# The heads of C in every second unit, and two keys on a partition in the values of B

## The chip, the cores and the metric

The kernel is one program on one NeuronCore of a Trainium2 chip. Five engines run their own instruction streams and wait for each other through semaphores: TensorE (PE, the matrix engine), VectorE (DVE), ScalarE (ACT), GpSimd (POOL) and SyncE (SP), which here only issues DMAs. TensorE reads SBUF and writes PSUM, eight banks of 512 f32 columns on 128 partitions. The metric is the device time of one execution in microseconds; lower is better. The profile is of one execution of its own.

## The reference, cut to what matters

Two layers of a decoder run over 256 prompt tokens and over 8 sequences of 8 new tokens, each with 1024 past positions. Token mixing has three head groups, A (6 heads, dilated window), B (6 heads, keys chosen by an indexer) and C (4 heads, two softmax maps each). The new tokens attend over caches; those of B and C lie in pages of 128 positions:

```python
def paged_rows(pool):
    rows = pool[l, page_table]
    return rows.reshape((nb, past) + rows.shape[3:])
...
kc_all = jnp.concatenate([paged_rows(cache_c_k), kc], axis=1)
vc_all = jnp.concatenate([paged_rows(cache_c_v), vc], axis=1)
oc = diff_attend(qc, kc_all, vc_all, q_pos, lam_l, lam_init, subln_g_l, rel_bias)
...
s = jnp.einsum('bthmd,bshmd->bhmts', q.astype(jnp.float32) * D_C ** -0.5, k_all.astype(jnp.float32))
s = jnp.where(dist >= 0, s + bias[None, :, None], -jnp.inf)
p = jax.nn.softmax(s, axis=-1)
...
a = p[:, :, 0] - lam_full * p[:, :, 1]
o = jnp.einsum('bhts,bshd->bthd', a, v_all.astype(jnp.float32))
```

A and B are of the same shape, with one map: softmax of q times the keys plus a bias, times the values. The order of the positions within a softmax and its sum of values doesn't matter, as long as both use the same. All is f32.

## The kernel before, in words

A layer runs in this order: projections (`PROJ`), with tiles of the adaLN matmuls between them; the units, which are the subject here; the output projection (`mix_out`, L1386) and norm; the MLP (L1085, L1524). All tiles of weights come through a ring of four slots on SP's queue.

**Units.** The 16 units of a layer (`UNITS`) do the new tokens' attention over the caches. Units 0 to 7 take the six heads of A for sequence n, units 8 to 15 (`second`) the six of B for sequence n - 8. A chunk is 128 features, that is two heads; a unit has three chunks of A or B and, as the fourth, one of the two chunks of C: heads 0 and 1 beside A, 2 and 3 beside B. A chunk's queries are 32 columns (`G`) of `qs`, gathered by GpSimd and zero where a head's features aren't, so that one matmul does both heads.

- `turn(u)` (L1297, L1298, L1306): TensorE transposes the exponentiated logits `S`, eight pages of 128 keys and the new keys, into PSUM; ScalarE (first pass) or VectorE (second) copies them to `ptbuf` (`turned_unit`).
- `logits(u+1)` (L1277): for each half of the keys (`q` 0 and 1) four matmuls of 512 columns, one for each chunk, into partitions 32c to 32c + 31 (`psf[G * c:G * c + G]`); then, as `q` 2, four of 8 columns for the new keys, after a wait for `u_nset`. For B the selection is added by L1284, one matmul for each chunk and q.
- one item of the prompt's attention (L1366, L1351, L1376), of which `SLOTS` says which unit takes which.
- `values(u)` (L1321): for each page and the new keys (`vs`) four matmuls of 128 columns into partitions 32c to 32c + 31 of bank 3.
- in the first seven units half of a late projection tile (L1397), `turn_out` (L1328), the other half. Before each waits `i_logit`, the item's maxima from VectorE.
- `turn_out(u)` waits for `u_oset`, which VectorE's `read_outputs` gives (L1830, L1832, L1834: the sum's reciprocal, and the output scaled by it), and turns the outputs back; VectorE's `place_outputs` copies them to `oT` and frees the bank for the next turn.

SP issues the loads of a unit's keys when the logits of unit n - 2 are through, and of its values when the values of n - 2 are; there are two buffers for everything, `s` = n mod 2. C's pages are read in rows of 512 bytes, half of the 1024 bytes that a position has, since a unit takes one chunk of two; ScalarE issues some of these loads in the second pass.

`LATE` has eight projection tiles; tile 0 is done ahead of unit 0, tile n + 1 in unit n. At the program's start three matmuls at L1149 make the bias table: the first two write partitions 0 to 15 of bank 0 and of bank 1, with 512 columns each, the third partitions 32 to 47 with 135 columns (`dist_ps_at`).

```python
def dist_ps_at(c):

    p0, (u0, u1) = 32 * (c // 2), DIST[c]
    return bank[c % 2][p0:p0 + H, 0:u1 - u0]
```

## Time and profile before

| | |
|---|---|
| median of 3 runs | 1382.98 us (1381.21 to 1383.24) |
| profiled execution | 1387.83 us |
| its span in the profile | 1386.0 us, 23151 instructions |
| TensorE busy | 1300.4 us, 94% |
| VectorE, ScalarE, GpSimd busy | 496.0, 258.4, 59.6 us |
| read from and written to HBM | 354.20 MB, 58.40 MB |

A row of a view gives the line, the engine, the operation, out<-in by names, stationary rows*columns, moving rows x columns, the type and the number of records. A matmul of f32 leaves two MATMUL records, a transpose one. Records of one line that follow each other are merged in a timeline; its second number is the stretch from the first's start to the last's end, so the distance between two rows' starts says best how long a group took. In a record's duration is also the time through the array, so concurrent and pipelined records overlap. `PEclk` is the granted clock as a share of 2.4 GHz.

### The profile page before, as it was taken

Reading aid. Unit: us, or ns where it says so; the run is one execution under the profiler, and the core shown is the slowest. Engines: PE = TensorE matmul, PEld = TensorE weight load, DVE = VectorE, ACT = ScalarE, POOL = GpSimd, SP = SyncE. Lnnn points to the kernel's source line nnn. Section 1 sums busy time; section 2 is a strip of 40 time slices with the busy share of each in tenths; the row PEclk is TensorE's granted clock in tenths of the full one; section 3 lists DMA queues with packets and bytes.
Section 4 is the critical chain, followed back from the end, with each engine's and each line's share of the span. In section 5 each row is a group of like instructions: output and inputs, shape, how many; then the busy total and the mean of one; then the engine's idle time right before and its main releaser. Section 6 shows DMA issues by size and latency. Waiting matters only on the chain.

```text
span 1386.0 us, 23151 instructions
## 1 busy us (share of the span) xinstructions
PE 1300.4 (94%) x8038; PEld 809.5 (58%) x8038; DVE 496.0 (36%) x1444; ACT 258.4 (19%) x647; POOL 59.6 (4%) x265
## 2 busy tenths in 40 slices
PE   5988899988999999999999999999899999999998
PEld 2544356644566666666666444665456667767775
DVE  1102458876664111011112056777756411101113
ACT  0111124422213110000003212443220311100001
POOL 1000000000001000000001000000000100000000
PEclk9999899998999999999999999999899999999999
DMA  9989989999943768877863687999994366676663
GB/s 350 226 277 260 274 292 370 329 333 347 300 167 111 277 232 299 314 272 262 331 222 138 205 292 276 332 331 349 349 349 173 129 244 212 221 284 212 212 212 137
DMA packets 189646, 363.83 MB, mean 262 GB/s; under 512 B 22928, under 2 KB 140440, under 8 KB 187866
## 3 DMA queue, kind: packets, MB, share of 16 engines
q1 hardware_dynamic: 155040, 345.62, 72.4%
q10 hardware_dynamic: 34490, 16.74, 5.0%
q8 instruction: 64, 1.05, 0.3%
q14 instruction: 52, 0.43, 0.1%
HBM read 354.20 MB, written 58.40 MB: 298 GB/s over the span
## 4 chain that ended last, share of the span: by engine, by line
PE 76%; DVE 9%; DMA 6%; DVEq 3%; issue 2%; ACT 2%; SPq 2%; ACTq 0%
PE psf L1085 22%; PE psf L1524 19%; DMA ring<-in_tiles 5%; PE psf L1386 4%; PE psf L1436 4%; PE psf L1321 3%; PE psf L1277 3%; PE psf L1507 3%; PE psf L1102 2%; PE psf L1397 2%; PE psf L1132 1%; PE psf L1351 1%; PE psf L1164 1%; DVE ranks L1708 1%; DVEq L1711 1%
## 5 line engine op out<-in xcount | busy, mean ns | idle before, releaser
L1085 PE MATMUL psf<-hT,ring 128*128 128x320 f32 x1184 | 328.8, 437 | 3.5 <-DMA ring<-in_tiles 3.2
L1085 PEld LDWEIGHTS psf<-hT,ring 128*128 128x128 f32 x1184 | 224.0, 191 | 111.2 <-issue 15.9
L1524 PE MATMUL psf<-big,ring 128*128 128x320 f32 x1024 | 278.9, 433 | 4.1 <-DVE big L1981 2.1
L1524 PEld LDWEIGHTS psf<-big,ring 128*128 128x128 f32 x1024 | 193.5, 190 | 90.4 <-issue 5.5
L1981 DVE TENSOR_TENSOR big<-sq 128x320 f32<-128x320 f32 x64 | 31.5, 492 | 248.8 <-ACT sq L1054 248.5
L1622 DVE TENSOR_SCALAR rstd<-psf,adaT 128x256 f32<-128x256 f32 x32 | 15.4, 482 | 250.1 <-PE psf L1524 234.9
L1012 ACT ACTIVATE sq<-xT 128x320 f32<-128x320 f32 x32 | 15.0, 470 | 321.5 <-DVE xT L1626 321.5
L1386 PE MATMUL psf<-oT,ring 128*128 128x320 f32 x256 | 71.6, 435 | 2.2 <-DVE oT L1844 1.0
L1054 ACT ACTIVATE sq<-psf 128x320 f32<-128x320 f32 x64 | 28.0, 437 | 238.9 <-PE psf L1085 224.6
L1277 PE MATMUL psf<-big,qs 128*32 128x512 f32 x512 | 66.7, 616 | 3.7 <-ACT zT L858 2.2
L1321 PE MATMUL psf<-big,ptbuf 128*32 128x128 f32 x2048 | 65.9, 283 | 0.1
L1436 PE MATMUL psf<-ring,hT 128*128 128x512 f32 x128 | 62.2, 631 | 0.0
L1102 PE MATMUL psf<-ring,cz 128*32 128x512 f32 x336 | 49.5, 626 | 12.9 <-DVE cz L1558 8.7
L1386 PEld LDWEIGHTS psf<-oT,ring 128*128 128x128 f32 x256 | 47.8, 190 | 23.5 <-DVE xT L1626 1.8
L1321 PEld LDWEIGHTS psf<-big,ptbuf 128*32 128x32 f32 x2048 | 56.4, 114 | 7.1 <-issue 4.4
L1569 DVE TENSOR_REDUCE adaT<-psf 128x36 f32<-128x144 f32 x24 | 7.3, 304 | 140.6 <-PE psf L1112 140.1
L1792 DVE CUSTOM_DVE_ANT_0 S<-psf,sbias 128x1032 f32<-128x1032 f32 x32 | 39.3, 1229 | 38.2 <-PE psf L1277 18.6
L858 ACT ACTIVATE zT<-psf,zscale 128x320 f32<-128x320 f32 x40 | 20.7, 528 | 162.1 <-PE psf L1085 70.3
L1708 DVE MAX8 ranks<-workbuf 128x8 f32<-128x520 f32 x64 | 44.9, 702 | 3.8
L1710 DVE MATCH_REPLACE8 workbuf<-ranks,workbuf 128x520 f32<-128x520 f32 x64 | 43.8, 684 | 0.3 <-issue 0.3
L1436 PEld LDWEIGHTS psf<-ring,hT 128*128 128x128 f32 x128 | 24.2, 200 | 31.6 <-issue 31.6
L1507 PE MATMUL psf<-hT,big 128*128 128x320 f32 x128 | 38.2, 463 | 2.9 <-ACT hT L1029 2.9
(212 smaller groups left out, 1303.3 us busy)
## 6 DMA issues: line engine op xcount, KB each, us to landing
ring<-in_tiles SPq DMA_DIRECT2D x266, 512.0 KB, 4.7
big<-in_cache_a SPq DMA_DIRECT2D x64, 768.0 KB, 7.2
out_cache_a<-in_cache_a SPq DMA_DIRECT2D x64, 768.0 KB, 6.2
big<-in_pool_bk SPq DMA_DIRECT2D x128, 192.0 KB, 5.3
big<-in_pool_bv SPq DMA_DIRECT2D x128, 192.0 KB, 6.9
big<-in_pool_cv SPq DMA_DIRECT2D x192, 64.0 KB, 5.4
big<-in_pool_ck SPq DMA_DIRECT2D x128, 64.0 KB, 4.5
big<-in_pool_ck ACTq DMA_DIRECT2D x128, 64.0 KB, 5.3
```

Source lines behind the costliest of these rows:

```text
L1085: ins = pe.matmul(ps[:, 0:T], ring[:, s, k, :], rhs[:, k, :], start=k == 0, stop=k == KD - 1)
L1102: ins = pe.matmul(bank[3][G * g:G * g + G, :], cz[:, c, :], wide(tile, kk), start=c < 4, stop=c >= 4)
L1277: ins = pe.matmul(psf[G * c:G * c + G, 512 * q:512 * q + w], qs[:, u.s, G * c:G * c + G], rhs, start=True, stop=not masked)
L1321: ins = pe.matmul(bank[3][G * c:G * c + G, 0:P], lhs, rhs, start=j == 0, stop=j == NPG)
L1386: ins = pe.matmul(wo_bank(m)[:, 0:T], ring[:, s, k, :], oT[:, AT_O[k], :], start=k == 0, stop=k == KD - 1)
L1436: ins = pe.matmul(bank[v_bank(g, tt)], hT[:, 2 * s + kk, P * tt:P * tt + P], wide(ring[:, slot], kk), start=first, stop=last)
L1507: ins = pe.matmul(up_bank(m)[:, 0:T], spare[m][:, k, :], hT[:, k, :], start=k == 0, stop=k == KD - 1)
L1524: ins = pe.matmul(bank[6 + m % 2][:, 0:T], ring[:, s, k, :], uT[:, KD * q + k, :], start=q + k == 0, stop=q == 3 and k == KD - 1)
L1708: dve.max(eight, work)
L1710: dve.match_replace(work, eight, work, TAKEN)
L1792: dve.tensor_tensor_reduce(out=S[:, 0, :], in0=psf[:, 0:L], in1=sbias[u.second][:], scale=1.0, scalar=-3e38, op0=ALU.add, op1=ALU.max, acc ...
L1981: dve.tensor_tensor(uT[:, i, :], sq[:, i % 2, :], sq[:, i % 2, :], ALU.mult).then_inc(up_set.sem, 1)
```

## The change

A unit is now light (n even) or heavy (n odd). A light unit has the three chunks of A or B alone, on 64 rows of queries; a heavy one these and both chunks of C, for its own sequence, on 128 rows. In the second pass the sequences are swapped in pairs (`n % NB ^ 1`), so that each sequence is heavy once. The table `QUAD` gives the 32 partitions of a chunk's result: chunks 0 and 2 share partitions 0 to 31, chunk 1 has 32 to 63, and C's two chunks 64 to 95 and 96 to 127. In the logits chunk 2 accumulates on chunk 0's result, its queries lying in other rows; in the values it gets a bank of its own, bank 4, same partitions.

C has one buffer for keys and one for values, loaded for heavy units only, in whole rows of 1024 bytes; GpSimd gathers C's queries for these alone. In the second pass the page of values, of B and of C, is read as 64 partitions with two neighbouring positions each (`load_rows`: 3072 and, for C, 2048 bytes in one piece); two pages fill 128 partitions, and the turn takes the odd and even columns of `S` apart (`page`). The first pass reads the values of A and C, and both passes all keys, in the plain order.

Further edits: tile 1 of `LATE` is done ahead of unit 0 too, so unit n takes tile n + 2; the first unit with two items is 10 and not 11; the C heads' norm (`gn`) is split in prompt and new tokens and not by chunk; the bias rows of C are loaded with one DMA for two maps; and the wait for the free output bank stands ahead of the lower half's turn only in heavy units, in light ones ahead of the values. The diff's core (`...` where lines are left out):

```diff
+C_W = NPG * 2 * P
+QUAD = [0, 1, 0, 2, 3]
+Q_STEP, Q_ROWS = 40, [0, G, 2 * NT]
...
-        self.n, self.b, self.s, self.second = n, n % NB, n % 2, n >= NB
-        self.q, self.k, self.qc, self.kc = (QB, KB, QC + 1, KC + 1) if self.second else (QA, KA, QC, KC)
-        self.v, self.vc = (VB, VC + P) if self.second else (VA, VC)
+        self.n, self.s, self.second, self.heavy = n, n % 2, n >= NB, n % 2 == 1
+        self.b = n % NB ^ 1 if self.second else n
+        self.q, self.k = (QB, KB) if self.second else (QA, KA)
+        self.v = VB if self.second else VA
...
-SLOTS = [*([n] for n in range(11)), [11, 12], [13], [14], [15], [ITEMS]]
+        self.chunks = [0, 1, 3, 4, 2] if self.heavy else [0, 1, 2]
+        self.rows = P if self.heavy else 2 * G
+        self.q_at = 3 * G if self.heavy else 0
+        self.at = 2 * A_W if self.heavy else 0
+    def q_of(self, c):
+        at = self.q_at + ((0, Q_STEP, 2 * G)[c] if c < 3 else G * c)
+        return slice(at, at + G)
...
+SLOTS = [*([n] for n in range(10)), [10, 11], [12], [13], [14], [15], [ITEMS]]
...
+            def load_rows(l, at, pool, dst, signal):
+                for j in range(NPG):
+                    sp.dma_start(dst[64 * (j % 2):64 * (j % 2) + 64, j - j % 2:j - j % 2 + 2, :]
+                                 .rearrange("p e w -> p (e w)"),
+                                 pool[ds(at[j] + l * N_PHYS, 1)].rearrange("o (p e) w -> (o p) (e w)", e=2)
+                                 ).then_inc(signal, 16)
...
             def load_b(l, u, at, half):
-                load_pages(l, at, a["pool_bv" if half else "pool_bk"], 0, (k_in, v_in)[half][u.s], (ld_k, ld_v)[half][u.s])
...
+                if half:
+                    load_rows(l, at, a["pool_bv"], v_in[u.s], ld_v[u.s])
+                else:
+                    load_pages(l, at, a["pool_bk"], k_in[u.s], ld_k[u.s])
...
-                    if d in (6, 7):
-                        at = pages(0, CHECKED) if d == 6 else at
-                        load_c(l, UNIT[0], at, d - 6)
...
-                        load_c(l, UNIT[1], at, d - 13)
+                        load_c(l, at, d - 13)
...
-                        load_c(l, u, at, 0)
...
+                        if u.heavy:
+                            load_c(l, at, 0)
...
-                    load_c(l, then, was, 1, range(NPG // 2 if then.second else NPG))
+                        if then.heavy:
+                            load_c(l, was, 1)
...
-                        for c in range(4):
...
+                        for c in u.chunks:
                             if q < 2:
                                 rhs = (k_in[u.s][:, 4 * q:4 * q + 4, P * c:P * c + P] if c < 3
-                                       else ck_in[u.s][:, 4 * q:4 * q + 4, :])
+                                       else ck_in[:, 4 * q:4 * q + 4, P * (c - 3):P * (c - 3) + P])
...
-                                rhs = zT[:, u.k + c if c < 3 else u.kc, t0:t0 + NT]
-                            masked = u.second and c < 3
-                            ins = pe.matmul(psf[G * c:G * c + G, 512 * q:512 * q + w], qs[:, u.s, G * c:G * c + G], rhs,
-                                            start=True, stop=not masked)
-                            if q == 2 and not masked:
-                                ins.then_inc(u_s.sem, 1)
+                                rhs = zT[:, u.k + c if c < 3 else KC + c - 3, t0:t0 + NT]
+                            masked, g = u.second and c < 3, G * QUAD[c]
+                            ins = pe.matmul(psf[g:g + G, 512 * q:512 * q + w], qs[:, u.q_of(c)], rhs,
+                                            start=c != 2, stop=c != 0 and not masked)
+                            if q == 2 and c and not masked:
...
-                            for c in range(3):
+                            for g in (0, G):
...
-                                ins = pe.matmul(psf[G * c:G * c + G, 512 * q:512 * q + w], selB[half, u.b, :],
+                                ins = pe.matmul(psf[g:g + G, 512 * q:512 * q + w], selB[half, u.b, :],
...
-                    pe.sem_inc(passed, 1)
-                    z0 = TS - NT - NT * u.b
-                    for j in range(NPG // 2, NPG):
-                        pe.transpose(bank[3 + j // 4][:, P * (j % 4):P * (j % 4) + P], S[:, 0, P * j:P * j + P], ident[:])
-                    pe.transpose(bank[2][0:TS, 256:384], znew[:, z0:z0 + TS], ident[:])
-                    if u.n:
-                        pe.wait_ge(u_out.sem, u_out.free(l, u.n))
-                    else:
+                    if u.n == 0:
                         pe.wait_ge(z_set.sem, z_set.done(l, MADE_AT[LATE[0]]))
                     pe.sem_inc(passed, 1)
+                    r, z0 = u.rows, TS - NT - NT * u.b
+                    page = lambda j: (S[0:r, 0, 2 * P * (j // 2) + j % 2:2 * P * (j // 2) + 2 * P:2] if u.second
+                                      else S[0:r, 0, P * j:P * j + P])
+                    for j in range(NPG // 2, NPG):
+                        at = P * j - 512 if u.heavy else r * j
+                        ins = pe.transpose(bank[4][:, at:at + r], page(j), ident[0:r, 0:r])
+                    pe.transpose(bank[2][0:TS, 256:256 + r], znew[0:r, z0:z0 + TS], ident[0:r, 0:r])
+                    if u.heavy:
+                        pe.wait_ge(u_out.sem, u_out.free(l, u.n))
+                        pe.sem_inc(passed, 1)
                     for j in range(NPG // 2):
-                        ins = pe.transpose(bank[3 + j // 4][:, P * (j % 4):P * (j % 4) + P], S[:, 0, P * j:P * j + P], ident[:])
+                        ins = pe.transpose(bank[3 if u.heavy else 4][:, r * j:r * j + r], page(j), ident[0:r, 0:r])
                     ins.then_inc(u_tp.sem, 1)
...
                 def values(u):
...
                     pe.wait_ge(u_tset.sem, u_tset.done(l, u.n))
+                    if u.n == 0:
+                        pe.wait_ge(z_set.sem, z_set.done(l, MADE_AT[LATE[1]]))
+                    elif not u.heavy:
+                        pe.wait_ge(u_out.sem, u_out.free(l, u.n))
...
-                        for c in range(4):
+                        for c in u.chunks:
+                            g = G * QUAD[c]
                             if j < NPG:
-                                lhs = PT[:, j, G * c:G * c + G]
-                                rhs = v_in[u.s][:, j, P * c:P * c + P] if c < 3 else cv_in[u.s][:, j, :]
+                                lhs = ptbuf[:, u.rows * j + g:u.rows * j + g + G]
+                                rhs = v_in[u.s][:, j, P * c:P * c + P] if c < 3 else cv_in[:, j, P * (c - 3):P * (c - 3) + P]
                             else:
-                                v0 = u.v + P * c if c < 3 else u.vc
-                                lhs, rhs = PT[0:TS, j, G * c:G * c + G], vs[0:TS, v0:v0 + P]
-                            ins = pe.matmul(bank[3][G * c:G * c + G, 0:P], lhs, rhs, start=j == 0, stop=j == NPG)
-                            if j == NPG:
-                                ins.then_inc(u_o.sem, 1)
+                                v0 = u.v + P * c if c < 3 else VC + P * (c - 3)
+                                lhs, rhs = PT[0:TS, j, g:g + G], vs[0:TS, v0:v0 + P]
+                            ins = pe.matmul(bank[4 if c == 2 else 3][g:g + G, 0:P], lhs, rhs, start=j == 0, stop=j == NPG)
+                            if j == NPG and c:
+                                ins.then_inc(u_o.sem, 1 if u.heavy else 2)
...
                 def turn_out(u):
                     pe.wait_ge(u_oset.sem, u_oset.done(l, u.n))
-                    pe.matmul(bank[3][:, P:P + 64], osb[:], turnO[:], start=True, stop=True).then_inc(u_ot.sem, 1)
+                    r, w = u.rows, 10 * NT if u.heavy else 4 * NT
+                    pe.matmul(bank[3][:, 256:256 + w], osb[0:r, 0:P], turnO[0:r, 0:w], start=True, stop=True)
+                    pe.matmul(bank[3][:, 256 + 4 * NT:256 + 6 * NT], osb[0:r, P:2 * P], ident[0:r, 2 * NT:G],
+                              start=True, stop=True).then_inc(u_ot.sem, 1)
...
-                chunk(MID[l][0], late_bank(0), hT)
+                pe.wait_ge(ada_set, 1 + max(ada_group(t) for t in PROJ[l] if t[0] in ("mix", "mlp")))
+                for i in range(2):
+                    chunk(MID[l][i], late_bank(i), hT)
...
-                    if u.n + 1 < len(LATE):
+                    if u.n + 2 < len(LATE):
...
-                        i = u.n + 1
+                        i = u.n + 2
...
                 def read_outputs(u):
...
-                    dve.tensor_scalar(osb[:], bank[3][:, 0:P], rs[:, u.s, 0:1], par_all[:, l, P_COEF:P_COEF + 1],
-                                      ALU.mult, ALU.mult).then_inc(u_oset.sem, 1)
+                    dve.tensor_scalar(osb[r, 0:P], bank[3][r, 0:P], rs[r, u.s, 0:1], par_all[r, l, P_COEF:P_COEF + 1],
+                                      ALU.mult, ALU.mult)
+                    dve.tensor_scalar(osb[0:G, P:2 * P], bank[4][0:G, 0:P], rs[0:G, u.s, 0:1], None, ALU.mult
+                                      ).then_inc(u_oset.sem, 1)
...
-                        first = bank[3][q, P + NT * half:P + NT * half + NT]
-                        ins = dve.tensor_copy(oT[q, u.o:u.o + 4, t0:t0 + NT],
-                                              bass.AP(first.tensor, first.offset, [list(first.ap[0]), [2 * NT, 4], [1, NT]]))
+                        turned = bank[3][q, 256:256 + 10 * NT].rearrange("p (c e t) -> p c e t", e=2, t=NT)[:, :, half]
+                        if u.heavy:
+                            dve.tensor_copy(oT[q, 3:8:4, t0:t0 + NT], turned[:, 3:5])
+                        ins = dve.tensor_copy(oT[q, u.o:u.o + 3, t0:t0 + NT], turned[:, 0:3])
```

How the instructions stand. TensorE in the first pass of layer 0, before: the end of unit 1's turn, the logits of unit 2, an item's turn and logits, the values of unit 1.

```order
L1298 MATMUL psf<-ident,znew 64x128
L1306 MATMUL psf<-ident,S 128x128 x4
L1277 MATMUL psf<-big,qs 32x512 x8
L1277 MATMUL psf<-zT,qs 32x8 x4
L1366 MATMUL psf<-ident,S 128x128 x2
L1351 MATMUL psf<-zT 128x256 x4
L1321 MATMUL psf<-big,ptbuf 32x128 x32
L1321 MATMUL psf<-vs,ptbuf 32x128 x4
```

TensorE at the same place in the changed kernel, from the logits of unit 2, a light one; the values are those of unit 1, a heavy one.

```order
L1313 MATMUL psf<-big,qs 32x512 x6
L1313 MATMUL psf<-zT,qs 32x8 x3
L1414 MATMUL psf<-ident,S 128x128 x2
L1399 MATMUL psf<-zT 128x256 x4
L1366 MATMUL psf<-big,ptbuf 32x128 x40
L1366 MATMUL psf<-vs,ptbuf 32x128 x5
```

TensorE one unit on: the turn of light unit 2, the logits of heavy unit 3, an item, and the values of unit 2.

```order
L1338 MATMUL psf<-ident,S 128x64 x4
L1339 MATMUL psf<-ident,znew 64x64
L1345 MATMUL psf<-ident,S 128x64 x4
L1313 MATMUL psf<-big,qs 32x512 x10
L1313 MATMUL psf<-zT,qs 32x8 x5
L1414 MATMUL psf<-ident,S 128x128 x4
L1399 MATMUL psf<-zT 128x128 x2
L1366 MATMUL psf<-big,ptbuf 32x128 x24
L1366 MATMUL psf<-vs,ptbuf 32x128 x3
```

What moved: of eight cache logits in each unit six stand in a light one and ten in a heavy one, of 32 cache values 24 and 40, and a light unit's turn moves 64 columns.

TensorE in the second pass of layer 0, before: the logits of unit 13 with the selection's matmuls (`sel`, `selB`).

```order
L1277 MATMUL psf<-big,qs 32x512 x4
L1284 MATMUL psf<-sel,selB 32x512 x3
L1277 MATMUL psf<-big,qs 32x512 x4
L1284 MATMUL psf<-sel,selB 32x512 x3
L1277 MATMUL psf<-zT,qs 32x8 x4
L1284 MATMUL psf<-sel,selB 32x8 x3
```

The same in the changed kernel, unit 13 being heavy.

```order
L1313 MATMUL psf<-big,qs 32x512 x5
L1320 MATMUL psf<-sel,selB 32x512 x2
L1313 MATMUL psf<-big,qs 32x512 x5
L1320 MATMUL psf<-sel,selB 32x512 x2
L1313 MATMUL psf<-zT,qs 32x8 x5
L1320 MATMUL psf<-sel,selB 32x8 x2
```

What moved: the logits of a half of the keys are five (in a light unit three), and the selection's matmuls two and not three.

VectorE in the second pass of layer 0, before: `read_outputs` and the start of `place_outputs` of unit 10.

```order
L1830 TENSOR_TENSOR rs<-sm 128x1
L1832 RECIPROCAL rs<-rs 128x1
L1834 TENSOR_SCALAR osb<-psf,rs,par_all 128x128
L1844 COPY oT<-psf 64x4x8 x2
```

The same in the changed kernel, unit 10 being light.

```order
L1883 TENSOR_TENSOR rs<-sm 64x1
L1885 RECIPROCAL rs<-rs 64x1
L1887 TENSOR_SCALAR osb<-psf,rs,par_all 64x128
L1889 TENSOR_SCALAR osb<-psf,rs 32x128
L1901 COPY oT<-psf 64x3x8 x2
```

What moved: a second scaled copy, of 32 partitions, stands between the first and the placing.

## Rows read from the trace of the kernel before

**Rows 1.** The page: busy us and share of each engine; the chain's shares.

```profile
PE 1300.4 (94%) x8038; PEld 809.5 (58%) x8038; DVE 496.0 (36%) x1444; ACT 258.4 (19%) x647; POOL 59.6 (4%) x265
...
PE 76%; DVE 9%; DMA 6%; DVEq 3%; issue 2%; ACT 2%; SPq 2%; ACTq 0%
```

**Rows 2.** Timeline of TensorE, a unit of the first pass: start, stretch, group.

```profile
208.75 0.60 PE L1297 MATMUL psf<-ident,S 128*128 128x128 f32 x4
...
209.82 1.92 PE L1277 MATMUL psf<-big,qs 128*32 128x512 f32 x16
211.57 0.22 PE L1277 MATMUL psf<-zT,qs 128*32 128x8 f32 x8
211.72 0.44 PE L1366 MATMUL psf<-ident,S 128*128 128x128 f32 x2
...
213.51 1.95 PE L1321 MATMUL psf<-big,ptbuf 128*32 128x128 f32 x64
215.40 0.42 PE L1321 MATMUL psf<-vs,ptbuf 64*32 64x128 f32 x8
215.75 0.44 PE L1376 MATMUL psf<-adarow,vp 128*64 128x128 f32 x4
```

**Rows 3.** Groups by shape: busy us, mean ns | idle before them, releasers.

```profile
L1277 PE MATMUL psf<-big,qs 128*32 128x512 f32 x512 | 66.7, 616 | 3.7 <-ACT zT L858 2.2 <-DVE sel L1744 1.5
L1321 PE MATMUL psf<-big,ptbuf 128*32 128x128 f32 x2048 | 65.9, 283 | 0.1
...
L1834 DVE TENSOR_SCALAR osb<-psf,rs,par_all 128x128 f32<-128x128 f32 x32 | 13.1, 410 | 2.5
...
L1328 PE MATMUL psf<-turnO,osb 128*128 128x64 f32 x64 | 12.3, 273 | 10.1 <-DVE osb L1834 10.1
...
L1397 PE MATMUL psf<-hT,oT 128*128 128x320 f32 x32 | 9.6, 442 | 1.2 <-DVE nmxi L1862 1.2
L1397 PE MATMUL psf<-hT,wki 128*128 128x320 f32 x32 | 9.6, 442 | 2.1 <-DVE nmxi L1862 2.1
L1397 PE MATMUL psf<-hT,zT 128*128 128x320 f32 x32 | 9.6, 442 | 1.8 <-DVE nmxi L1862 1.8
...
L1277 PE MATMUL psf<-zT,qs 128*32 128x8 f32 x256 | 7.6, 180 | 4.0 <-DVE ptbuf L1908 4.0
```

**Rows 4.** Windows: stretch, length, busy PE PEld DVE ACT POOL, PEclk, DMA share, GB/s.

```profile
38.90:40.80 1.90, 1.90 (x11) 0.37 (x14) 1.18 (x3) 0.00 (x0) 0.00 (x0) 1.00 0.33 93
...
208.70:302.20 93.50, 87.34 (x1084) 56.01 (x1083) 72.86 (x242) 36.35 (x106) 9.03 (x48) 0.98 1.03 344
302.20:373.40 71.20, 63.16 (x803) 35.48 (x803) 47.14 (x166) 18.65 (x59) 4.51 (x24) 0.90 1.09 347
...
320.90:325.20 4.30, 4.30 (x75) 3.11 (x75) 0.90 (x6) 2.01 (x6) 0.00 (x0) 0.50 1.10 350
...
960.00:1045.00 85.00, 75.45 (x952) 43.48 (x946) 58.59 (x205) 21.50 (x69) 5.65 (x30) 0.92 1.07 341
```

**Rows 5.** Line L1149, ns min/median/max and forms; then the group in TensorE's timeline.

```profile
L1149 PE MATMUL psf<-big,relb x6: 275/589/600, 38.9 to 40.2; 34*16 34x512 f32 x4, 34*16 34x135 f32 x2
...
38.92 1.89 PE L1149 MATMUL psf<-big,relb 34*16 34x512 f32 x6
```

**Rows 6.** Timeline of TensorE, the selection's matmuls in a unit of B.

```profile
304.48 0.39 PE L1284 MATMUL psf<-sel,selB 64*32 64x512 bf16 x3
304.80 1.06 PE L1277 MATMUL psf<-big,qs 128*32 128x512 f32 x8
```

**Rows 7.** Timeline of TensorE, the values of two units of B.

```profile
308.92 1.95 PE L1321 MATMUL psf<-big,ptbuf 128*32 128x128 f32 x64
...
321.02 3.64 PE L1321 MATMUL psf<-big,ptbuf 128*32 128x128 f32 x64
```

**Rows 8.** The page, DMA queues (q1 by SP, q10 by ACT): packets, MB, share of 16 engines.

```profile
q1 hardware_dynamic: 155040, 345.62, 72.4%
q10 hardware_dynamic: 34490, 16.74, 5.0%
```

183 lines of the change are left out of this document (98 added, 85 removed).

## The prediction, as it was made

> **What bounds the kernel now.** I read the busy times and the chain of waits first. TensorE is busy 94% of the span and 76% of the chain that ended last is its own; VectorE is busy 36% [rows 1]. So I go to TensorE's timeline in the stretch that the change rewrites, the 16 units of each layer (197 to 386 us and 865 to 1052 us). A unit there is a train of TensorE groups with hardly a gap: turn 1.07 us (208.75 to 209.82), cache logits 1.75, logits of the new keys 0.15, the prompt item, cache values 1.89, new values 0.35 [rows 2]. All groups of the logits waited 3.7 and 4.0 us in the whole kernel, the values 0.1 us, and no DMA is among the releasers [rows 3]. The DMA engines are full there (share 1.03 and 1.09 of their time), but TensorE is busy 87.34 of 93.50 us and 63.16 of 71.20 us [rows 4]. The units run at TensorE's pace, with the transfers just ahead.
>
> **What the matmuls cost there.** Logits and values are matmuls with a stationary operand of 32 columns, so each fills one of four column strips of the array; where its result lies (partitions 0 to 31, 32 to 63, ...) says which. A matmul of f32 leaves two records. Eight cache logits of 512 columns (16 records, two for each strip and half of the keys, four a strip) take 1.75 us by their starts [rows 2]: 0.437 us for each record of a strip, four strips side by side. What happens when two such matmuls want the same strip is shown by the group at L1149: two of its three matmuls write partitions 0 to 15 of two different banks, with 512 columns each, that is four records in one strip, and the group takes 1.89 us at a full clock [rows 4, 5]. Take off the end of the last record, 0.59 us by the group's own records, and three steps of 0.43 us are left. Its third matmul lies in the next strip and adds nothing. So different strips overlap, and the same strip is a queue, whatever the bank.
>
> **The change, part by part.** *Logits.* Before, a unit puts one chunk on each strip. After, a light unit has chunks 0, 1, 2 on strips 0, 1, 0, and a heavy one chunks 0, 1, 3, 4, 2 on strips 0, 1, 2, 3, 0 (the table QUAD). Both have two rounds in strip 0 where there was one. The number of matmuls stays 8 in two units; the rounds double. Four records more in strip 0 at 0.437 us: +1.74 us a unit. The eight-column matmuls of the new keys took 0.15 us; a second round is between 0.05 and 0.15, I take 0.08.
> *Values.* 32 matmuls of 128 columns, 16 records a strip, take 1.89 us, 0.118 a record [rows 2]. Now 32 records stand in strip 0. If the strip sets the pace they take twice 1.89; if issue did, only the streamed columns count, 0.437 times 128/512 = 0.109 a record, 3.49 in all. So +1.60 to +1.89; I take 1.75, between these close ends. The new values took 0.35 us; a second round costs from two records (0.22) to 0.35, I take the lower, since 0.35 holds the change of form too. Together 1.74 + 0.08 + 1.75 + 0.22 = 3.79 us a unit, bounds 3.61 and 4.13, for 32 units: **+121.3 us** (115.5 to 132.2). All of it lies on TensorE, which nothing covers.
> *Masks.* In the units of B the selection's matmuls fill three strips side by side in 0.32 us (304.48 to 304.80) [rows 6]; now two, one round as before: 0.
> *Turns.* The 16 light units transpose 64 rows, not 128. Nine transposes take 1.07 us. At best half goes, 0.53 us; at worst nothing, since the stationary side keeps its 128 columns. I take 0.25: -4.0 us (0 to -8.5). By the Trainium skill (TensorE: Matmul & The Clock Gate, "LDWEIGHTS (loading the stationary operand)") a load's time goes by its columns and not by its rows, so 64 rows would load as slowly as 128. By that alone this term would be nearer 0 and the sum up to 4 us higher; no row here has a transpose of 64 rows.
> *Turning the outputs back.* A second matmul of 16 columns follows the first: at most the 0.15 us of the four eight-column ones, at least two records' 0.04; I take 0.10, +3.2 us. VectorE gets a second scaled copy of the output, 32 x 128, behind one of 410 ns [rows 3]. It raises the signal only after the second. TensorE waits for that signal in 16 units (10.1 us), those with no late projection tile around the turn-back; now there are 18, because one late tile moves ahead of the units. Bounds 0 and 0.41 us each; I take 0.3: +5.4, and 10.1/16 = 0.6 us for each of the two new ones, +1.2. In the other units two half tiles of 2.2 us hide it. Heavy units place two more heads' rows with two more copies; only the next light unit's values wait for that, some 5 us later: 0.
> *Waits that the longer trains swallow.* The second round gives 1.7 us before the eight-column logits wait for the turned new keys: 4.0 us go. It gives 2 us before the late tiles of home wkibuf, zT and oT wait for the item's maxima: 2.1 + 1.8 + 1.2 = 5.1 us go. The wait for the last projected tile, 2.2, and the one for the selection, 1.5, ahead of the first unit of B go too, since that tile comes a unit earlier and VectorE has more time [rows 3]. Together -12.8. What is late next is TensorE itself.
> *Clock.* Of 302 to 373 us the mean granted clock is 0.90, of 960 to 1045 us 0.92; within it stretches at 1.2 GHz, as 320.9 to 325.2, where the values took 3.64 us and not 1.95 [rows 4, 7]. They cost some 0.10 x 71 + 0.08 x 85 = 14 us in all, and the engine had idled ahead of them. With some of the idling gone I take -4 (0 to -14).
> *Transfers.* The bytes are the same; C comes as 1024-byte rows, and B's and C's values as longer runs. Nothing waits for a cache load, and each unit lasts longer: 0. C's buffer is now single, but a load starts when the last heavy unit's logits are through, two units (20 us or more) ahead of use. C for unit 0 is gone and that for unit 1 is double, ahead of the values' projection: -3 to +3, I take 0. POOL gathers less for light units, off the path.
> Sum: 121.3 - 4.0 + 3.2 + 6.6 - 12.8 - 4 = **+110.3 us**. The profiled execution took 1387.83 us, with a span of 1386.0; it becomes 1498. The median of the runs lies 4.85 below it, so the forecast is 1382.98 + 110.3 = **1493 us**. With all ends one way the sum is 115.5 - 8.5 + 1.3 - 12.8 - 14 - 3 = +79, or 1462; the other way, with half of the waits left, 132.2 + 4.8 + 8.6 - 6.4 + 3 = +142, or 1525.
>
> **Rivals.** *The strips are not what counts.* If two matmuls on one strip and different banks overlapped, or strip 0's second round slipped beside the next chunks, the change would keep the saved waits and turns alone: about -12, 1371. The L1149 group speaks against it, and strip 0 alone has twice the records.
> *The transfers set the units' pace (faster).* The queue issued by ScalarE has 34490 packets of 485 bytes on average in 5.0% of 16 engines' span, 32 ns each or 66 ns a kilobyte; the main queue pays 72.4% for 345.62 MB, 46 ns [rows 8]. C's 33.6 MB at the second rate and not the first save 0.66 ms of engine time, 41 us over 16 engines. If the share over 1 were the bound, the kernel would take 1342. It decides only where TensorE would wait for a load, and it waits for none; at +3.8 us a unit it waits still less. Of the 512-byte rows the Trainium skill (DMA: Bandwidth & Descriptors, "Specifications") says that 512 bytes already reach the line rate; by that even these 41 us would not be there, while the two queues' rates differ here by a third.
> *The clock falls in the light units.* In them one or two of four strips work for most of 7.5 us. If the chip then grants 1.2 GHz, as in [rows 7], each light unit loses up to 7.5 us; over half of the 16 it is 60 us, 1553. For it: nothing here shows how the clock takes an array three quarters empty. Against: L1149 ran so at a clock of 1.00, if only for 1.9 us.
> *More is hidden than I count*: other stalls shrink, light trains let items run beside them: 1440 to 1462.
>
> **How the numbers follow.** Forecast (1462 to 1525) 0.77, more hidden 0.06, clock 0.10, strips free 0.04, transfers 0.03. The range of 8 in 10 is 1460 to 1528. A measurement of this kernel can tell about 0.2% from no change. Faster by more: both last cases, 0.07. Within 0.2%: 0.01. Slower: 0.92.
>
> **What would show it.** In the profile after: cache logits of a unit 3.5 us by their starts in light and heavy units alike, values 3.5 to 3.8, the L1149 group unchanged; no wait of the logits for the turned new keys; the wait ahead of the turn-back near 0.9 us; units of 15 to 16 us in the first pass; a DMA share clearly under 1 in the units. Values of 1.9 us, or logits of 1.75, would prove the strips' rule wrong; a mean clock under 0.9 from 200 to 320 us would be the clock's case; a wait for ck, cv, k or v on TensorE would show that I misjudged the single buffer.

## The result, and the profile after

| | before | after |
|---|---|---|
| median, side by side | 1382.10 us (1376.99 to 1383.24, 4 runs) | 1507.51 us (1502.12 to 1510.52, 4 runs) |
| profiled execution, its span | 1387.83, 1386.0 us | 1502.12, 1500.3 us |

The ratio is 1.0911, with a 95% interval of 1.0868 to 1.0954: 125 us slower, against 110 forecast (1493, range 1460 to 1528). The profiled executions are 114.3 us apart, and the sum by steps below is made against these.

The page of after, its lines that answer [rows 1, 8]: busy times, the chain, the two queues.

```profile
PE 1416.1 (94%) x8054; PEld 886.3 (59%) x8054; DVE 499.8 (33%) x1501; ACT 253.9 (17%) x639; POOL 48.8 (3%) x202
...
q1 hardware_dynamic: 119216, 341.68, 67.8%
q10 hardware_dynamic: 21226, 20.93, 6.2%
...
PE 85%; DMA 8%; DVE 3%; issue 2%; ACTq 1%; DVEq 1%; SPq 1%; ACT 1%
```

TensorE has 116 us more of busy time with nearly as many records (8054 and 8038). The timeline of TensorE answers [rows 2]: a light unit's turn, the logits of the heavy unit behind it (20 records), the light unit's values, and later the heavy unit's values.

```profile
203.14 0.46 PE L1338 MATMUL psf<-ident,S 64*128 64x64 f32 x4
...
203.83 3.19 PE L1313 MATMUL psf<-big,qs 128*32 128x512 f32 x19
...
207.49 1.07 PE L1399 MATMUL psf<-zT 32*128 32x128 f32 x8
208.49 3.68 PE L1366 MATMUL psf<-big,ptbuf 128*32 128x128 f32 x48
212.10 0.62 PE L1366 MATMUL psf<-vs,ptbuf 64*32 64x128 f32 x6
...
215.00 0.41 PE L1374 MATMUL psf<-turnO,osb 64*128 64x32 f32 x2
215.25 0.37 PE L1375 MATMUL psf<-ident,osb 64*128 64x16 f32 x2
215.55 2.42 PE L1445 MATMUL psf<-hT,ring 128*128 128x320 f32 x8
...
224.33 3.68 PE L1366 MATMUL psf<-big,ptbuf 128*32 128x128 f32 x80
227.94 0.62 PE L1366 MATMUL psf<-vs,ptbuf 64*32 64x128 f32 x10
```

The heavy unit's logits take 3.66 us for cache and new keys together (203.83 to 207.49), where a unit's took 1.90; those of the next light unit take 3.66 as well (218.88 to 222.54). The values of a light unit (48 records) and of a heavy one (80) both take 3.61 us (208.49 to 212.10, 224.33 to 227.94), where 64 records took 1.89: only the 32 records that both have in strip 0 count.

TensorE's waits in the whole kernel: who waited for whom, us in total, times, longest.

```profile
PE psf L1374 <- DVE osb L1889: 13.0, 18, 0.9
PE psf L1313 <- issue: 9.4, 2, 4.7
...
PE psf L1313 <- DMA big<-in_pool_ck: 1.1, 3, 0.6
```

The waits for the turned new keys and for the items' maxima (4.0 and 5.1 us, [rows 3]) are gone. That ahead of the first unit of B is not: it was 2.2 + 1.5 and is now 4.7 in each layer. The profile names no releaser for it (`issue`); the timelines of TensorE and of VectorE there:

```profile
306.72 0.63 PE L1345 MATMUL psf<-ident,S 128*128 128x128 f32 x4
312.06 3.59 PE L1313 MATMUL psf<-big,qs 128*32 128x512 f32 x6 [4.70 <-issue]
```

```profile
307.87 0.48 DVE L1786 TENSOR_SCALAR sel<-workbuf,bound 128x520 bf16<-128x520 f32 x1
...
311.41 0.43 DVE L1794 TENSOR_SCALAR sel<-workbuf 128x520 bf16<-128x520 f32 x1
```

`select` makes `sel`, which the logits of unit 8 need. It stands in VectorE's program behind the placing of unit 6's outputs, and runs from 307.87 to 311.84; the logits start at 312.06. Before, a late projection tile stood around unit 6's turn-back on TensorE; it moved ahead of unit 0, and with it the cover.

Windows of after, columns as in [rows 4]. The stretch from 302 to 373 us lies in the second pass in all kernels here, but not at the same units:

```profile
302.20:373.40 71.20, 60.73 (x573) 35.40 (x571) 39.23 (x147) 14.27 (x50) 3.10 (x16) 0.92 0.97 251
...
203.00:300.00 97.00, 96.82 (x872) 62.80 (x871) 60.23 (x208) 29.02 (x86) 5.05 (x26) 1.00 0.77 272
```

In the first pass TensorE is busy 96.82 of 97 us at a clock of 1.00. In the second the DMA engines are as good as full (0.97) and yet bring 251 GB/s, where they brought 347 at 1.09. Over both queues, the kernel before paid (0.724 + 0.050) x 1386.0 x 16 = 17164 us of one DMA engine's time; after pays (0.678 + 0.062) x 1500.3 x 16 = 17764 for the same bytes. The experiments follow that up.

### The profile page after: what moved, and what is told of

Its sections match the earlier page's. It is cut to its first block, busy times and chain, and to the rows that moved or that the text cites. A ratio compares the mean times of both kernels' runs of the same rounds, so it can differ in the third digit from the quotient of the medians.

```text
span 1500.3 us, 22339 instructions
## 1 busy us (share of the span) xinstructions
PE 1416.1 (94%) x8054; PEld 886.3 (59%) x8054; DVE 499.8 (33%) x1501; ACT 253.9 (17%) x639; POOL 48.8 (3%) x202
## 4 chain that ended last, share of the span: by engine, by line
PE 85%; DMA 8%; DVE 3%; issue 2%; ACTq 1%; DVEq 1%; SPq 1%; ACT 1%
PE psf L1115 22%; PE psf L1574 18%; PE psf L1313 8%; PE psf L1366 7%; PE psf L1434 4%; DMA ring<-in_tiles 4%; PE psf L1445 4%; PE psf L1484 3%; DMA big<-in_pool_ck 3%; PE psf L1132 3%; PE psf L1557 2%; PE psf L1399 1%; PE psf L1162 1%; PE psf L1194 1%; PE psf L1220 1%
## 5 line engine op out<-in xcount | busy, mean ns | idle before, releaser
L1115 PE MATMUL psf<-hT,ring 128*128 128x320 f32 x1216 | 337.4, 437 | 2.0 <-DMA ring<-in_tiles 1.7
L1115 PEld LDWEIGHTS psf<-hT,ring 128*128 128x128 f32 x1216 | 230.3, 191 | 112.8 <-issue 12.9
L1313 PE MATMUL psf<-big,qs 128*32 128x512 f32 x512 | 128.2, 639 | 10.5 <-issue 9.4
L1366 PE MATMUL psf<-big,ptbuf 128*32 128x128 f32 x2048 | 117.8, 279 | 0.0
L1366 PEld LDWEIGHTS psf<-big,ptbuf 128*32 128x32 f32 x2048 | 109.2, 109 | 6.3 <-issue 4.2
L1844 DVE CUSTOM_DVE_ANT_0 S<-psf,sbias 64x1032 f32<-64x1032 f32 (+1 forms) x32 | 39.3, 1229 | 94.3 <-PE psf L1320 47.0
L1313 PEld LDWEIGHTS psf<-big,qs 128*32 128x32 f32 x512 | 26.7, 112 | 74.1 <-issue 72.8
L931 ACT ACTIVATE znew<-S,nmx 64x8 f32<-64x8 f32 (+1 forms) x32 | 9.6, 301 | 196.7 <-DVE nmx L1847 196.7
```

The lines of the kernel that those rows point to most:

```text
L1115: ins = pe.matmul(ps[:, 0:T], ring[:, s, k, :], rhs[:, k, :], start=k == 0, stop=k == KD - 1)
L1313: ins = pe.matmul(psf[g:g + G, 512 * q:512 * q + w], qs[:, u.q_of(c)], rhs, start=c != 2, stop=c != 0 and not masked)
L1366: ins = pe.matmul(bank[4 if c == 2 else 3][g:g + G, 0:P], lhs, rhs, start=j == 0, stop=j == NPG)
L1844: dve.tensor_tensor_reduce(out=S[r, 0, :], in0=psf[r, 0:L], in1=sbias[u.second][r, :], scale=1.0, scalar=-3e38, op0=ALU.add, op1=ALU.max, ...
```

## The experiments

Two theories stood at the start. *Strips:* the second round in strip 0 is the slowdown, and the rest is small. *More than strips:* taking rounds away doesn't give their time back, because the loads or another wait are just behind.

**The strips, put into the kernel before.** Chunk 2's values go to strip 0 of another bank, as the change has them; nothing else.

```diff
-                            ins = pe.matmul(bank[3][G * c:G * c + G, 0:P], lhs, rhs, start=j == 0, stop=j == NPG)
+                            o = 0 if c == 2 else G * c
+                            ins = pe.matmul(bank[4 if c == 2 else 3][o:o + G, 0:P], lhs, rhs, start=j == 0, stop=j == NPG)
```

> The kernel before with one thing of the change alone: the values of chunk 2 go to partitions 0 to 31 of bank 4 and not to 64 to 95 of bank 3, so two heads of each unit are missing from the output; all counts, loads and copies as before. Theory (strip queue): cache values 1.89 to 3.6 us and new values 0.35 to 0.55 in each of 32 units, +61 us, less 5 us for the three late tiles a layer that wait for the item's maxima: 1382 + 56 = 1438. Rival (strips don't count): 1382.

Measured: 1435.09 us (1431.92 to 1436.39), ratio 1.0352 (1.0322 to 1.0383). The values in TensorE's timeline:

```profile
216.44 3.68 PE L1322 MATMUL psf<-big,ptbuf 128*32 128x128 f32 x64
220.05 0.62 PE L1322 MATMUL psf<-vs,ptbuf 64*32 64x128 f32 x8
```

The same 64 records, 3.61 us and not 1.89, for a change of 32 partitions' place. A strip is one queue, whatever the bank. The time is 50 us above the 1384.87 of the kernel before beside it, near the 1438 expected.

**The strips, taken out of light units.** First the values, then the logits of chunk 2 go to strip 2, which light units leave idle; the results of chunk 2 there are not read, so its heads are missing from the output.

```diff
-                            ins = pe.matmul(bank[4 if c == 2 else 3][g:g + G, 0:P], lhs, rhs, start=j == 0, stop=j == NPG)
+                            o = 2 * G if c == 2 and not u.heavy else g
+                            ins = pe.matmul(bank[4 if c == 2 else 3][o:o + G, 0:P], lhs, rhs, start=j == 0, stop=j == NPG)
```

> The changed kernel, but in light units the values of chunk 2 go to partitions 64 to 95 of bank 4, a strip of their own, and not to strip 0; its result is then not read, so two heads of each light unit are missing from the output. Same count, shapes and order of instructions. Theory (two matmuls on one strip are a queue, whatever the bank): cache values of a light unit fall from 3.61 to about 1.9 us and its new values from 0.55 to 0.35, heavy units stay at 3.61: 16 x 1.9 = 30 us less than the changed kernel's 1507.5, about 1478. Rival (strips are not what counts, the column count or the issue of the records is): no difference, 1507.

```diff
-                            ins = pe.matmul(psf[g:g + G, 512 * q:512 * q + w], qs[:, u.q_of(c)], rhs,
-                                            start=c != 2, stop=c != 0 and not masked)
+                            apart = c == 2 and not u.heavy
+                            o = 2 * G if apart else g
+                            ins = pe.matmul(psf[o:o + G, 512 * q:512 * q + w], qs[:, u.q_of(c)], rhs,
+                                            start=c != 2 or apart,
+                                            stop=apart or (c != 0 or not u.heavy) and not masked)
```

> The changed kernel, but in light units the logits of chunk 2 go to partitions 64 to 95, a strip of their own, and are not read; two heads of each light unit are missing. Theory (strip queue): cache logits of a light unit, 3.48 us, fall to 1.75, new keys by 0.05 or so; 16 x 1.75 = 28 us less than 1507.5, about 1479, and a little less gained where the wait ahead of the first unit of B stays. Rival (accumulation on one result, not the strip, costs the time): the same fall here, but none in the kernel with the values spread. Rival (neither): 1507.

Measured: 1495.39 us (1484.89 to 1496.7), ratio 1.0768 (1.0721 to 1.0816), and 1493.2 us (1489.85 to 1499.62), ratio 1.0778 (1.0733 to 1.0823). Light values, light logits, and for the first kernel logits of a heavy unit in the second pass:

```profile
211.40 1.95 PE L1367 MATMUL psf<-big,ptbuf 128*32 128x128 f32 x48
...
351.01 3.59 PE L1313 MATMUL psf<-big,qs 128*32 128x512 f32 x10 [1.97 <-DMA big<-in_pool_ck]
```

```profile
220.09 1.92 PE L1315 MATMUL psf<-big,qs 128*32 128x512 f32 x12
```

The groups fell as the strips say, by 1.7 us in 16 units each, 28 us. The values fell too, though there the two results of strip 0 lie in different banks and don't accumulate, so it isn't accumulation that costs. By the medians only 12 and 14 came. The first kernel's waits for C's keys rose from 1.1 to 8.7 us in 4, and a slow clock follows them: the 3.59 us above are 1.90 at full clock. In the second kernel they are 2.6 us. The mean granted clocks are 0.968 and 0.970, where the changed kernel had 0.984 and, in another execution, 0.980: by an estimate 15 to 24 us of each kernel's time. So the strips are right where they rule, and something stands close behind them in the second pass.

**One round everywhere.** Chunk 2 has a strip of its own in light units and is left out in heavy ones.

```diff
+                            if c == 2 and u.heavy:
+                                continue
...
+                            apart = c == 2
+                            o = 2 * G if apart else g
+                            ins = pe.matmul(psf[o:o + G, 512 * q:512 * q + w], qs[:, u.q_of(c)], rhs,
+                                            start=True, stop=apart or not masked)
...
+                            o = 2 * G if c == 2 else g
+                            ins = pe.matmul(bank[4 if c == 2 else 3][o:o + G, 0:P], lhs, rhs, start=j == 0, stop=j == NPG)
```

> The changed kernel with one round everywhere: light units with chunk 2 on a strip of its own (logits and values), heavy units without chunk 2 at all; a third of A's and B's heads is missing from the output. Theory: TensorE loses the second round in all 32 units, 1.75 us of logits and 1.92 us of values each, 117 us in all, which would give 1391 if nothing else bound; with units of 10 to 12 us again the single buffer of C is loaded late (its keys take 13 us from issue to use in the second pass), so I expect waits of the heavy logits for ck of 1 to 3 us each in the second pass and 1395 to 1410. Rival (the transfers had set the pace before): near 1350 since C's rows are longer. Rival (the change's other parts cost more than the strips): well over 1410.

Measured: 1448.88 us (1446.06 to 1456.52), ratio 1.0471 (1.0427 to 1.0515). A miss of 39 to 54 us. A heavy unit's logits in the second pass, then light values behind them, then a window:

```profile
330.32 1.93 PE L1317 MATMUL psf<-big,qs 128*32 128x512 f32 x8 [4.65 <-DMA big<-in_pool_ck]
...
338.40 3.63 PE L1373 MATMUL psf<-big,ptbuf 128*32 128x128 f32 x48
...
302.20:373.40 71.20, 60.15 (x595) 32.82 (x592) 40.77 (x156) 15.18 (x52) 4.25 (x22) 0.76 1.08 264
```

With the strips out of the way the transfers count: a share of 1.08, 264 GB/s, TensorE's waits for C's keys 11.1 us and for B's keys 3.2, and behind such waits the clock of 1.2 GHz, 0.76 in the mean. Is it C's single buffer, or the way in which rows are read?

**Values in plain order.** In the changed kernel, and in the last one, B's and C's values of the second pass are read with one key on a partition, 128 partitions a page.

```diff
-                    load_rows(l, at, a["pool_bv"], v_in[u.s], ld_v[u.s])
+                    load_pages(l, at, a["pool_bv"], v_in[u.s], ld_v[u.s])
...
-                        act.dma_start(cv_in[64 * (j % 2):64 * (j % 2) + 64, j - j % 2:j - j % 2 + 2, :]
-                                      .rearrange("p e w -> p (e w)"),
-                                      a["pool_cv"][ds(at[j] + l * N_PHYS, 1)].rearrange("o (p e) w -> (o p) (e w)", e=2)
+                        act.dma_start(cv_in[:, j, :], a["pool_cv"][ds(at[j] + l * N_PHYS, 1)].rearrange("o p w -> (o p) w")
...
-                    page = lambda j: (S[0:r, 0, 2 * P * (j // 2) + j % 2:2 * P * (j // 2) + 2 * P:2] if u.second
-                                      else S[0:r, 0, P * j:P * j + P])
+                    page = lambda j: S[0:r, 0, P * j:P * j + P]
```

> The changed kernel with the values of B and C in the second pass read in the plain order again, one key on a partition, 128 partitions a page, and the turn taking the columns of S in their plain order; nothing else is different, and all is computed. Theory: TensorE's strip 0 sets the pace and the way in which values are read doesn't matter beside it: 1504 to 1508, the turn 0.13 us a unit shorter or longer, the stretch 306 to 430 as long as before this edit. Rival: the page on 64 partitions makes the transfers slow (253 GB/s at a share of 1.01 in the second pass, where the kernel before has 347 at 1.09), so that C's keys arrive late: then the rate at a full share is 320 or more or the share falls to 0.8, the 1.1 us of waits for C's keys go, and the time falls to 1497 to 1502.

> The kernel e3_one_round (chunk 2 on a strip of its own in light units; heavy units leave chunk 2's heads out in logits and values) with the values of B and C in the second pass read in the plain order. It tells what the 40 to 50 us are made of by which e3_one_round was slower than the strips alone say (1449, expected 1395 to 1410). If the loads on 64 partitions are what makes C's keys late (4.65 us of wait at 330, then a clock of 1.2 GHz over 300 to 390), the waits for C's keys (11.1 us in 2) and for B's (3.2) fall under 3 us, the mean clock of that stretch rises from 0.77 to 0.9, and the time is 1420 to 1430. If C's single buffer is the cause, loaded whole for one unit in two and late whatever its rows are, the waits stay and the time is 1442 to 1450.

Measured: 1499.34 us (1498.4 to 1502.42), ratio 1.0838 (1.0809 to 1.0868); and 1403.11 us (1399.49 to 1410.26), ratio 1.0147 (1.0105 to 1.019). The same window, first of the changed kernel with plain values, then of one round with plain values:

```profile
302.20:373.40 71.20, 60.90 (x568) 35.11 (x566) 41.35 (x156) 14.29 (x48) 3.13 (x16) 0.91 0.87 285
```

```profile
302.20:373.40 71.20, 62.78 (x736) 35.30 (x732) 47.22 (x179) 17.37 (x60) 4.29 (x22) 0.90 1.03 350
```

The pairs cost 46 us where strips don't rule (1448.88 to 1403.11), and 8 where they do (1507.51 to 1499.34, in different series). C's single buffer stays as it was in both, so it is not the cause of the 46. The rate went from 264 GB/s at a share of 1.08 to 350 at 1.03, and the waits for C's keys from 11.1 to 0.7 us. The last kernel was expected at 1420 to 1430 and came out better than that.

The edit has a second effect, on TensorE, which I had put at 0.13 us a unit at most: with plain values the turn no longer takes every second column of `S`. A light unit's turn in the second pass, first of the changed kernel, then with plain values, both at a clock of 1.00:

```profile
326.42 0.69 PE L1338 MATMUL psf<-ident,S 64*128 64x64 f32 x4
...
327.58 3.21 PE L1313 MATMUL psf<-big,qs 128*32 128x512 f32 x10
```

```profile
323.66 0.46 PE L1335 MATMUL psf<-ident,S 64*128 64x64 f32 x4
...
324.35 1.90 PE L1311 MATMUL psf<-big,qs 128*32 128x512 f32 x10
```

The turn takes 1.16 us with every second column and 0.69 without. In heavy units it is 1.28 (341.38 to 342.66) against 1.19 (336.56 to 337.75). Over 8 light and 8 heavy units that is an estimate of 4.5 us, so of the 8 us over half is the turn and not the loads, and of the 46 a tenth.

**The pairs, put into the kernel before.** B's values as the change reads them; C's chunk, whose rows stay 512 bytes, in the same order.

```diff
-                load_pages(l, at, a["pool_bv" if half else "pool_bk"], 0, (k_in, v_in)[half][u.s], (ld_k, ld_v)[half][u.s])
+                    for j in range(NPG):
+                        sp.dma_start(v_in[u.s][64 * (j % 2):64 * (j % 2) + 64, j - j % 2:j - j % 2 + 2, :]
+                                     .rearrange("p e w -> p (e w)"),
+                                     a["pool_bv"][ds(at[j] + l * N_PHYS, 1)].rearrange("o (p e) w -> (o p) (e w)", e=2)
+                                     ).then_inc(ld_v[u.s], 16)
```

> The kernel before with one part of the change alone: in the units of B the values of B (3072 bytes in one piece) and of C's chunk (two pieces of 512 bytes) lie with two neighbouring keys on a partition, 64 partitions a page, and the turn takes the columns of S apart. All is computed. If long rows are cheaper for the transfers, the share in 302 to 373 us falls under 1.0 and the time stays at 1383 to 1385, since nothing waits for them, or 1380 if there is something hidden. If a load on 64 partitions is slower, the rate in that stretch falls from 347 to some 260 GB/s, waits for k, v or C's loads appear on TensorE, which has none now, and with the slow clock behind them the time is 1395 to 1420. The turn with a stride of two columns alone costs at most 0.2 us in 16 units, 3 us.

Measured: 1431.27 us (1425.07 to 1435.83), ratio 1.035 (1.0312 to 1.0389). One row of the timeline, the first two of this kernel's waits for loads, the window, and the queues:

```profile
335.80 3.64 PE L1336 MATMUL psf<-big,ptbuf 128*32 128x128 f32 x64 [3.50 <-DMA big<-in_pool_cv]
...
PE psf L1336 <- DMA big<-in_pool_cv: 15.6, 6, 3.5
...
PE psf L1290 <- DMA big<-in_pool_ck: 6.8, 2, 4.5
...
302.20:373.40 71.20, 56.15 (x647) 33.07 (x646) 35.58 (x124) 14.30 (x48) 4.52 (x24) 0.79 1.12 267
...
q1 hardware_dynamic: 146848, 345.62, 73.5%
q10 hardware_dynamic: 34490, 16.74, 5.8%
```

By the queues' lines the same bytes cost (0.735 + 0.058) x 1423.3 x 16 = 18059 us of one engine, 895 more than before; between the changed kernel and its version with plain values it is 17764 - 16858 = 906. Both concern 33.6 MB: some 27 ns a kilobyte more, on top of 46 to 47. In ScalarE's queue packets and bytes are those of before [rows 8], and its time rose from 1109 to 1321 us. Of its packets only C's values, still 512 bytes each, go to 64 partitions; but the next run shows that not all of the rise is theirs. The time is above the 1395 to 1420 expected. The longest waits, 15.6 us, are for C's values in a form that the changed kernel doesn't have (there they come as 2048 bytes), so the 47 us are the price of this kernel's pairs; the 46 above are those of the change's own.

The Trainium skill (SBUF — State Buffer, "Door 1: The DMA port swizzle") says that partitions 0 to 63 are reached through eight of sixteen ports and 64 to 127 through the other eight, so that a load to 64 partitions is as slow as one to 32. These runs agree in direction, with a time per byte that rose by about a half (27 on 47 ns); they don't show the ports.

**64 partitions or long rows.** In the kernel before each load of a page of B's values brings half of it, to 64 partitions, in rows of 1536 bytes as before.

```diff
+                        p = slice(64 * (j % 2), 64 * (j % 2) + 64)
+                        sp.dma_start(v_in[u.s][p, j, :], a["pool_bv"][ds(at[j] + l * N_PHYS, 1), p, :]
+                                     .rearrange("o p w -> (o p) w")).then_inc(ld_v[u.s], 16)
```

> The kernel before, where each load of a page of B's values brings only half of it: 64 keys to 64 partitions (0 to 63 or 64 to 127 in turn), rows of 1536 bytes as before, so that 12.6 MB of 345.6 on SP's queue are left out and the outputs of B's heads are wrong by that. It tells whether b4_pair_rows was slow because of 64 partitions or because of the rows' new length. The main queue's time was 0.724 x 1386 x 16 = 16055 us in the kernel before, 46 ns a kilobyte, and 16738 in b4_pair_rows, which moves the same bytes; put down to B's values (25.2 MB) and C's (4.2 MB) that is 23 ns a kilobyte more, 69. If the number of partitions is the cause, the halved loads cost 69 ns a kilobyte: 16055 - 1158 + 869 = 15766 us, a queue share of 71.1%, and the share of all in 302 to 373 us falls from 1.09 to 0.98. If the rows' length was the cause, they cost 46 still: 15476 us, 69.8%, and 0.88. The time stays at 1380 to 1386 by both, since the values of before wait for nothing.

Measured, one run of each: 1391.53 us, where before had 1380.14 beside it. The queue and the window:

```profile
q1 hardware_dynamic: 146848, 333.04, 70.5%
...
302.20:373.40 71.20, 61.22 (x765) 34.83 (x765) 44.20 (x156) 18.33 (x57) 4.38 (x24) 0.88 0.91 244
```

The queue's time is 0.705 x 1389.7 x 16 = 15676 us, between the two expectations: by this queue alone the 12.6 MB left cost 62 ns a kilobyte, against 46 in full loads and 69 expected of 64 partitions, 16 of 23 ns. But ScalarE's queue, at a share of 5.4%, rose as well, from 1109 to 1201 us, though this edit leaves its loads as they were. With full loads it was 1078 to 1109 us in three kernels (the one before, that with the values stacked, that with the early selection). This one run thus suggests that loads to 64 partitions make the other queue's packets longer too, so both queues have to be counted. Together they take 16877 us, where 17164 less 12.6 MB of full loads would be 16585: some 23 ns a kilobyte more for the 12.6 MB left, beside the 27 of the pairs. By this run most of the pairs' cost goes with the number of partitions, at an unchanged row length. The shares are given to 0.1%, which is 2 to 3 ns here; whether the longer rows add the rest stays open.

The time was expected unchanged and is 11 us up with 12.6 MB less to move. Two waits for B's keys are 2.0 of them. The mean granted clock is 0.980 where the run beside it had 0.985, some 7 more. TensorE's waits for weights ahead of the output projection are 5.6 us, where the trace of before has 0.8. With one run of each the sum of these can't be closed, and why the clock was lower stays open.

**C in whole rows, undone.** The changed kernel with C's pages read in two DMAs of 512-byte rows, save the paired values of the second pass.

```diff
-                load_pages(l, at, a["pool_cv" if half else "pool_ck"], (ck_in, cv_in)[half], (ld_ck, ld_cv)[half])
+                for j in range(NPG):
+                    for e in range(2):
+                        sp.dma_start(dst[:, j, P * e:P * e + P], pool[ds(at[j] + l * N_PHYS, 1), :, P * e:P * e + P]
+                                     .rearrange("o p w -> (o p) w")).then_inc(signal, 16)
```

> The changed kernel with C's pages fetched in halves again: each page of keys, and of values in the first pass, as two DMAs with rows of 512 bytes (C's values of the second pass keep their 2048 bytes). Same bytes, twice the packets and issues for them. Theory (TensorE sets the pace in the units, and row length is off the path): within 2 us of the changed kernel, save for the heavy logits of the second pass, which already wait up to 0.6 us for ck and may wait 1 to 3 us each: +0 to +10. Rival (the longer rows gained what the profile doesn't show, 41 us of transfers by the queues' rates): +20 to +40.

Measured: 1525.96 us (1521.94 to 1529.03), ratio 1.1025 (1.0998 to 1.1051), 18 us above the changed kernel.

```profile
367.83 3.59 PE L1319 MATMUL psf<-big,qs 128*32 128x512 f32 x10 [7.29 <-DMA big<-in_pool_ck]
...
q1 hardware_dynamic: 137648, 341.69, 67.6%
q10 hardware_dynamic: 30442, 20.93, 6.6%
```

The queues' time is 18056 us, 292 more for 25.2 MB: 12 ns a kilobyte. The 18 us lie between the two expectations. Whole rows help, and in the changed kernel they count. That they count because the pairs have brought the transfers close to the bound is argued and not tested, and the edit also doubles the number of DMAs issued for these pages, which no run takes apart.

**The selection earlier.** In the changed kernel `select` follows `rank` in unit 5; in the kernel before the same, together with ScalarE's copy of a late tile ahead of its issues of C's loads.

```diff
                         rank()
-                    if n == NB - 2:
                         select()
```

> The changed kernel with VectorE's selection (five instructions, 3.9 us) moved one unit up, from the end of unit 6 to the end of unit 5, right behind the ranking whose result it needs. Theory (TensorE idles 4.7 us ahead of unit 8's logits because the selection stands behind unit 6's output copies and the late tile that used to cover it is gone): that idle goes to under 1 us in both layers, and the stretch at 1.2 GHz behind it too (unit 8's logits took 7.0 us there and 4.3 us in unit 10): 2 x (4.7 + 2.7) = 10 to 15 us less than the changed kernel. Rival (the logits wait there for the keys of unit 8 or for the last projected tile): no change, under 2 us.

> The kernel before with two moves and nothing of the change: VectorE's selection one unit up, as in the run with the early selection, and ScalarE's copy of the late projection tile ahead of its issues of C's loads and not behind them. Theory: the idle of 2.2 us (layer 0, for the projected tile) and 1.5 us (layer 1, for the selection) ahead of unit 8's logits go, and in layer 0 the slow clock behind it, which cost about 2.5 us: 4 to 7 us less than before, 1376 to 1379. Rival (the next wait takes their place, the item's or the new keys'): within 2 us of before.

Measured: 1500.59 us (1497.18 to 1511.32), ratio 1.085 (1.0818 to 1.0882), where the changed kernel had 1508.38 (1504.52 to 1509.71), ratio 1.0893 (1.0868 to 1.0917), in the same series; and 1399.08 us (1394.93 to 1404.64), ratio 1.0109 (1.0083 to 1.0135).

> The changed kernel again, unedited, beside the next three on the same chip, so that differences under a per cent can be read: 1.091 times the kernel before, 1500 to 1511 us.

The first logits of B in the changed kernel with the early selection:

```profile
310.75 0.63 PE L1345 MATMUL psf<-ident,S 128*128 128x128 f32 x4
...
311.31 1.90 PE L1313 MATMUL psf<-big,qs 128*32 128x512 f32 x6
```

The 4.70 us are gone, and the logits behind them run in 1.90 and not 3.59 us: that the selection was what they waited for is shown. The medians differ by 8 us where 10 to 15 were expected, with intervals that overlap a little, so what it is worth in time is not settled. The version of the kernel before was expected at 1376 to 1379 and is slower than that kernel. The waits of 2.2 and 1.5 us ahead of unit 8 are gone in it, but there is this one of TensorE's:

```profile
PE psf L1277 <- ACT ptbuf L953: 13.9, 4, 4.0
```

It comes from the other move. ScalarE's issues of C's loads used to run while it would have waited for the late tile's matmuls. Now they stand behind that tile's copy and straight ahead of the copy of the turned new keys of units 6 and 7: eight issues of keys from 268.19, 3.92 us, and the copy at 272.22. No version here is faster than the kernel before.

## Why the prediction was right, point by point

| step | forecast | in the traces |
|---|---|---|
| second round in strip 0 | +121.3 | +116.8 |
| turns of 64 rows | -4.0 | -4.1 |
| second matmul of the turn-back | +3.2 | +9.0 |
| wait ahead of it | +6.6 | +2.9 |
| waits for the new keys and maxima | -9.1 | -9.1 |
| wait ahead of unit 8 | -3.7 | +5.7 |
| clock | -4 | -6.5 |
| sum | +110.3 | +114.7, of 114.3 |

The sum is close in part by luck. Against the forecast the steps are off by -4.5, -0.1, +5.8, -3.7, 0, +9.4 and -2.5 us, and these errors cancel down to +4.4.

*The strips* carried the forecast, and the runs bear them out from both sides: +50 us when values alone are stacked in the kernel before (1435.09 against the 1384.87 beside it), 96 us between the kernels with two rounds and with one, values plain in both (1499.34 - 1403.11). In the trace it is 1.76 + 1.92 us a unit in the first pass and 1.70 + 1.92 in the second. The rival that strips are free is out.

*The turns* took 0.69 us (203.14 to 203.83), not 1.07, in light units of the first pass, and 0.13 less than before in the second, where they take every second column: 8 x 0.38 + 8 x 0.13 = 4.1. The agreement with 4.0 hides two errors: 64 rows save more than the 0.25 us taken, and the columns apart, which the prediction didn't price, take 0.47 us a unit of it back. The weight loads of these transposes took 138 ns with 64 rows and 141 with 128 in the first pass, so the saving doesn't lie in them. With every second column they took 208 ns.

*The turn-back* is the term that was too small by three times. The second matmul has 16 columns, but it costs as the first does: 0.25 and 0.30 us (215.00, 215.25, 215.55). It loads 128 stationary columns, in two loads of 0.19 us each, where a load of 32 takes 0.11; that these loads set the price is read from the trace and not tested. Before, the next group began 0.17 us behind the only one, as TensorE's timeline of the kernel before shows:

```profile
206.37 0.33 PE L1328 MATMUL psf<-turnO,osb 128*128 128x64 f32 x2
206.54 2.37 PE L1397 MATMUL psf<-hT,ring 128*128 128x320 f32 x8
```

I had priced it by the eight-column matmuls, whose stationary side has 32 columns. From the first matmul's start to the next group's, 0.17 us became 0.55 in light and 0.37 in heavy units of the first pass, and 0.28 became 0.55 in the second: 8 x 0.38 + 8 x 0.20 + 16 x 0.27 = 9.0. The wait ahead of it was priced at +0.3 us and rose by 0.1 (10.1 us in 16 to 13.0 in 18). The scaled copy of 32 partitions takes 329 ns, but it starts ahead of the first one's end: VectorE's chain from the sum to the last copy took 0.88 us before (291.49 to 292.37) and 1.12 after (304.38 to 305.50).

*The wait ahead of unit 8* failed by its sign, 9.4 us of sum. The prediction said that it goes, "since that tile comes a unit earlier and VectorE has more time". But VectorE begins `select` behind unit 6's output copies (306.20), which hang on TensorE's turn-back of that very unit, so it had no more time; and the tile that moved had been the cover. I had followed what the moved tile gives, and not what stood behind it. The run with the early selection shows the wait's cause, by making it vanish.

*The transfers* came out near the forecast 0 only because the strips hid them. I had taken the two keys on a partition for free, or better for their longer runs; alone in the kernel before they cost 47 us (1431.27 against 1383.92), and in the changed one 8, of which by the estimate 4.5 are the turn's. The prediction's rival saw only the saving from whole rows: at 12 ns a kilobyte it is there, 18 us in the changed kernel, and the pairs take 27 ns a kilobyte back. "Nothing waits for a cache load" was true of the kernel before; 1.1 us of waits for C's keys after showed how near they were. Of the prediction's signs, a DMA share clearly under 1 in the units came in the first pass (0.77) and not in the second (0.97). A wait for C's keys was to show that the single buffer was misjudged; but a second profiled execution of the changed kernel has none, nor has the version with plain values and the same buffer. What was misjudged is the pairs.

*The clock* did not fall in light units: 1.00 in the first pass, with two of four strips idle all through a light unit's logits and values. That rival is out. The clock falls behind idle stretches, as at unit 8. The mean granted clock of the profiled spans is 0.978 before and 0.984 after: 0.022 x 1386 = 30.5 us and 0.016 x 1500 = 24.0, so -6.5, an estimate that takes all of the time to go by the clock.

The medians lie 11 us further apart than the profiled executions, from both sides. The profiled execution of before is 5.7 us above its median (1387.83 against 1382.10), and that of after 5.4 below (1502.12 against 1507.51). After's three other runs are at 1506 to 1511, with a mean granted clock of 0.977 to 0.979 and not 0.984; 0.6% of 1500 is 9 us, enough for the 5.4. For the 5.7 the record has no clocks of the other runs. The medians' distance of 125.4 stands for the change; the steps account for 114.3 of it.

## What to carry to other kernels

Count matmuls by the 32-column strip in which their results lie, not by their number: two in one strip are a queue, also in different banks, and an idle strip is worth nothing to them. A load to half of the partitions can be slower by a half per byte, longer rows or not; read GB/s beside the DMA share, since a full share at a falling rate is what shows it. When an item of work moves, ask what it had been covering (the late tile, and ScalarE's issues), and when a term is hidden by the term you are adding, price it alone too: the two costs here (50 for the values alone, and 47) did not add up, and neither comes back fully when only one is undone.

## What the hardware showed that I had not expected

- A kilobyte took 47 ns of a DMA engine's time over both queues in the kernel before. By the differences between runs it took some 70 (47 + 23) in loads to 64 partitions with rows of 1536 bytes, and some 74 (47 + 27) in the pairs; part of this shows in the packets of the other queue.
- A transpose that takes every second column of its input is slower: four of 64 rows took 0.53 us (326.42 to 326.95), against 0.29 in plain order (323.66 to 323.95).
- The strips run ahead of each other past the program's order. In the light unit's logits below, the new keys' matmul of chunk 1, alone on its strip, starts at 221.49, ahead of the last record of the cache keys at 221.91, which stands before it in the program.

```profile
218.88 3.19 PE L1313 MATMUL psf<-big,qs 128*32 128x512 f32 x11
221.49 0.23 PE L1313 MATMUL psf<-zT,qs 128*32 128x8 f32 x2
221.91 0.59 PE L1313 MATMUL psf<-big,qs 128*32 128x512 f32 x1
222.34 0.27 PE L1313 MATMUL psf<-zT,qs 128*32 128x8 f32 x4
```

- A transpose of 64 rows is cheaper than one of 128: four took 0.30 us (203.14 to 203.44, the next group's start), where four of 128 rows took 0.44.
- A wait of some us can cost more than itself: behind 4.70 us of idling the next six records' group took 3.52 us and not 1.83, at a clock of 1.2 GHz (0.50 from 312.06 to 315.58). It was so too behind waits of 1.97, 3.50, 4.65 and 7.29 us.
